# A hybrid encoder layer on eight cores: rewriting a phase-by-phase kernel as prioritised work streams, with a time-phased depthwise conv, a block-major last down pass, one weight ring and norm sums on VectorE

## What is computed

```python
x = x + 0.5 * swiglu(rmsnorm(x, ffn1_norm), ffn1_gate, ffn1_up, ffn1_down)     # hidden width 2816
z = rmsnorm(x, mix_norm) @ w_in                                               # 2560 columns
q, k, v, u = z[..., :512], z[..., 512:1024], z[..., 1024:1536], z[..., 1536:]
attn_out = chunk_band_attention(q, k, v, rel_bias)       # 8 heads of 64; 64-frame chunks see themselves and 8 before
g = u[..., :512] * sigmoid(u[..., 512:])
dw = causal_depthwise_conv(g, dw_kernel) + dw_bias       # 512 channels, 31 taps
conv_out = silu(layernorm(dw, conv_ln_g, conv_ln_b))     # norm over the channels
x = x + concat([attn_out, conv_out]) @ w_out
x = x + 0.5 * swiglu(rmsnorm(x, ffn2_norm), ffn2_gate, ffn2_up, ffn2_down)
y = rmsnorm(x, final_norm)
```

## Time and profile before

| what | us |
|---|---|
| median of 6 runs | 1756.24 (1752.36 to 1757.49) |
| the profiled execution | 1751.98 |
| its span on the slowest core (all cores: 1743.4 to 1750.4) | 1750.4 |
| TensorE busy | 1574.9 (90%) |
| VectorE busy | 569.3 (33%) |
| ScalarE busy | 459.0 (26%) |
| mean granted TensorE clock of the cores | 0.943 to 0.950 |

### The profile page before, as it was taken

One profiled execution on the slowest core, in us unless ns is written; L12 is line 12 of the kernel. 1 busy time (PEld: TensorE's weight loads), 2 busy tenths in 40 slices (PEclk: granted clock), 3 DMA queues, 4 the chain that ended last, 5 costly groups with the idle time before them and its releaser, 6 DMA issues.

```text
span 1750.4 us, 23671 instructions; the slowest of 8 cores (1743.4 to 1750.4 us)
## 1 busy us (share of the span) xinstructions
PE 1574.9 (90%) x8732; PEld 824.5 (47%) x8732; DVE 569.3 (33%) x1457; ACT 459.0 (26%) x874; POOL 47.8 (3%) x94
## 2 busy tenths in 40 slices
PE   4999999798877899959999998999898769999996
PEld 1555555344334455524555554444344435555552
DVE  3222222523444322243222223324354452222224
ACT  4110110313363311133110112223545351100113
POOL 0000000000000000000000000000000000000000
PEclk9999999899888899978999999899998969999998
DMA  9543324324000564661333232231000022333113
GB/s 224 85 72 61 55 49 79 85 49 73 1 1 10 88 103 85 111 171 49 65 59 65 49 73 49 42 66 31 1 1 1 1 48 49 70 63 55 25 27 124
DMA packets 14943, 105.68 MB, mean 60 GB/s; under 512 B 1648, under 2 KB 1776, under 8 KB 5872
## 3 DMA queue, kind: packets, MB, share of 16 engines
q0 software_dynamic: 12960, 83.89, 27.2%
q1 hardware_dynamic: 1872, 20.28, 3.3%
HBM read 179.66 MB, written 8.39 MB: 107 GB/s over the span
## 4 chain that ended last, share of the span: by engine, by line
PE 82%; DVE 6%; ACT 6%; DMA 3%; issue 3%; ACTq 0%; DVEq 0%; SPq 0%; POOLq 0%
PE ps L359 40%; PE ps L393 18%; PE ps L645 6%; PE ps L448 3%; PE ps L743 3%; PE ps L489 3%; PE ps L574 2%; DMA xres<-xin 2%; PE ps L467 2%; PE ps L600 2%; ACT sq L318 2%; PE ps L320 1%; DVE diag L629 1%; DVE scr L333 1%; DVE xres L333 1%
## 5 line engine op out<-in xcount | busy, mean ns | idle before, releaser
L359 PE MATMUL ps<-scr,gur 128*128 128x512 bf16 (+1 forms) x3872 | 693.0, 342 | 1.3 <-DVE scr L333 1.3
L359 PEld LDWEIGHTS ps<-scr,gur 128*128 128x128 bf16 x3872 | 380.1, 98 | 313.3 <-issue 10.0
L393 PE MATMUL ps<-scr,dr 128*128 128x512 bf16 (+1 forms) x1936 | 352.7, 344 | 2.7 <-DMA dr<-wdB 1.2
L367 ACT ACTIVATE scr<-ps 128x512 f32<-128x512 f32 (+1 forms) x242 | 125.7, 519 | 734.4 <-PE ps L359 734.4
L370 DVE TENSOR_TENSOR scr<-ps,scr 128x512 bf16<-128x512 f32 (+1 forms) x242 | 143.9, 595 | 534.4 <-PE ps L359 529.2
L393 PEld LDWEIGHTS ps<-scr,dr 128*128 128x128 bf16 x1936 | 189.9, 99 | 161.4 <-issue 7.6
L398 DVE SCALAR_TENSOR_TENSOR xres<-ps,xres 128x512 f32<-128x512 f32 (+1 forms) x176 | 103.9, 594 | 230.0 <-PE ps L393 229.9
L320 PE MATMUL ps<-sq,cb_sb 128*128 128x512 bf16 (+1 forms) x176 | 67.2, 409 | 87.8 <-ACT sq L318 83.9
L318 ACT ACTIVATE sq<-xres 128x512 bf16<-128x512 f32 (+1 forms) x176 | 88.1, 544 | 193.9 <-PE ps L320 137.6
L645 PE MATMUL ps<-g,diag 128*128 128x512 bf16 (+1 forms) x620 | 123.1, 361 | 5.9 <-DVE diag L629 5.9
L600 PE MATMUL ps<-scr,V 128*128 128x256 bf16 (+3 forms) x288 | 59.3, 309 | 48.3 <-DVE scr L616 22.9
(11 more groups left out here) (66 smaller groups left out, 570.4 us busy)
## 6 DMA issues: line engine op xcount, KB each, us to landing
gur<-wgu POOLq DMA_DIRECT2D x44, 1024.0 KB, 9.4
dr<-wdA POOLq DMA_DIRECT2D x16, 768.0 KB, 7.9
dr<-wdB POOLq DMA_DIRECT2D x16, 640.0 KB, 6.4
gur<-win POOLq DMA_DIRECT2D x10, 1024.0 KB, 9.4
xres<-xin SPq DMA_DIRECT2D x4, 2048.0 KB, 11.2
yout<-xres SPq DMA_DIRECT2D x3, 2048.0 KB, 6.3
gur<-wout POOLq DMA_DIRECT2D x4, 1024.0 KB, 9.5
xres<-xin SPq DMA_DIRECT2D x2, 1024.0 KB, 15.8
```

The source lines that it names most:

```text
L359: P.op("pe", lambda h, bank=bank, lhsT=lhsT, rhs=rhs, kc=kc: h.matmul(bank, lhsT=lhsT, rhs=rhs, start=(kc == 0), stop=(kc == 7)), reads=(( ...
L367: P.op("act", lambda h, tt=tt, gb=gb: h.activation(out=tt, in_=gb, func=AF.Silu), reads=(("ps", bG),), writes=(("tmpF", ti),))
L393: P.op("pe", lambda h, bank=bank, lhsT=lhsT, rhs=rhs, fl=fl, nf=nf: h.matmul(bank, lhsT=lhsT, rhs=rhs, start=(fl == 0), stop=(fl == nf - 1 ...
```

## The change

The kernel is written anew. Each phase is now a Python generator, a stream with a priority; `Sched.run` asks the streams in the order of priority whether their next piece of work can start by a planned time that `Prog` keeps for every engine (each operation comes with a planned duration), emits the first that can, or else the one that can soonest. The order on every engine is still fixed when the program is built.

- The passes' blocks are now 512, 384 and 384 frames (`GROUPS`). The second group's streams have priorities 10 lower in rank, so that its first feed-forward work can stand inside the first group's last.
- Conv: the gated values are written as four time phases (`gT`), 64 copies from SBUF to SBUF on SyncE's queue per group (32 on the way in, 32 back) bring 4 phases x 32 channels onto the partitions (`gp`), and 9 matmuls per 32 channels replace 31 per 128, each on a quarter of the frames. The weights for it (`wcv`) are made on the host and loaded like the others; nothing builds diagonals on VectorE. Its channel statistics lie on all phases at once, and a copy on VectorE brings the result back into time order (`cvt`).
- Norms: ScalarE squares each slice right behind the operation that completes it, VectorE adds the squares, one matmul with ones per block sums over the partitions.
- The last down part of each feed-forward runs block by block over all 8 output tiles. The final norm writes into a buffer of its own (`yb`), which is stored from there.
- Attention: the scores of two heads lie in four joined PSUM banks, and one exponential takes both heads; the streams of projections and of the output projection fill in.
- All weights go through one ring of 17,408 columns in the order of use. The first block of frames is loaded ahead of the weights, the other two behind the first weight piece.

```diff
-            for kc in range(8):
-                i = nxt("sq", 2)
...
-                P.op("pe", lambda h, bank=bank, sqt=sqt, kc=kc: h.matmul(
-                    bank, lhsT=onesS, rhs=sqt, start=(kc == 0), stop=(kc == 7)),
...
+GROUPS = (((512, True), (384, False), (384, False)),
+          ((512, False), (384, False), (384, False)))
...
+            now = self.P.t["pe"] + 0.1
+            best = None
+            for s in self.streams:
+                r = s[3]()
+                if r <= now:
+                    best = (r, s)
+                    break
+                if best is None or r < best[0]:
+                    best = (r, s)
...
+        def square(st, g, kc, s):
...
+            act(sqt, xsl(g, kc, s), AF.Square, n, (xk,), (("sq", i),))
+            if k < 7:
+                dve(lambda h: h.tensor_tensor(out=ss, in0=ss, in1=sqt, op=ALU.add), n,
+                    (("ssum", r), ("sq", i)), (("ssum", r),))
...
+                if hf == 0:
+                    order = [(dg, s, dm2) for dg in range(4) for s in blocks for dm2 in range(2)]
+                else:
+                    order = [(dg, s, dm2) for s in blocks for dg in range(4) for dm2 in range(2)]
...
+                for s4 in range(4):
+                    for j in range(4):
+                        src = gT[32 * j:32 * j + 32, 2 * pc:2 * pc + 2, s4, 0:W]
...
+            for grp in range(16):
+                p = wp[(gi, "cv%d" % (grp // 4))]
...
+                    if ("gp", gi) not in F or (grp > 1 and ("cstat", gi, grp - 2) not in F):
+                        return INF
...
+                for d in range(9):
+                    mm(b, 0, wv[:, grp % 4, d, :], gp[:, grp, 8 - d:8 - d + U], U, d == 0, d == 8,
+                       (("w", p.id), ("gp", grp), "gph"), d == 8)
...
+                act(abq[:, i, 0:U], a, AF.Copy, U, (("acc", grp),), (("abq", i),))
+                act(abq[:, i + 1, 0:U], a, AF.Square, U, (("acc", grp),), (("abq", i + 1),))
...
+            for grp in range(16):
+                gcol = cs[:, CS_LNG + grp:CS_LNG + grp + 1]
+                bcol = cs[:, CS_LNB + grp:CS_LNB + grp + 1]
+                act(co[:, grp, 0:U], acc[:, grp, 0:U], AF.Silu, U, (("acc", grp),), (("co", grp),),
+                    bias=bcol, scale=gcol)
...
+                    act(Pb[:, pi, :, 0:w], src, AF.Exp, 2 * w, (("ps", 2 * sp_), ("ps", 2 * sp_ + 1)), (("P", pi),))
...
+                def rdy0():
+                    if ("Q", gi, s) not in F or ("v", gi, s) not in F or ("ln45", gi) not in F:
+                        return INF
...
+        for g in G:
+            q = 10 * g.gi
+            S.add(q + 2, ffn(g, 0))
+            S.add(q + 3, glu(g))
+            S.add(q + 4, proj_k(g))
+            S.add(q + 5, attention(g))
+            S.add(q + 4.5, conv(g))
+            S.add(q + 6, proj_v(g))
+            S.add(q + 7, proj_q(g))
+            S.add(q + 8, wout(g))
+            S.add(q + 9, ffn(g, 1))
```

1588 lines of the change are left out of this document (902 added, 686 removed).

## The result

The changed kernel takes 1616.2 us (median of ten runs) against 1755.8 us of the kernel before: a ratio of 0.9205, 95% interval 0.9196 to 0.9215. That is faster, as forecast, but by 140 us and not by 263, and 56 us above the upper end of the range. The profiled execution took 1616.9 us, with a span of 1615.4 us on its slowest core. In some executions one die, or both, runs at a lower granted clock and the time is longer (one of 1730.8 us for this kernel); medians and comparisons leave these out.

A forecast was written before the change was run, and what follows sets the result against it. TensorE was taken as the bound. Start 27, feed-forward stretches 1059.8 and other stretches 401.4 us sum to a span of 1488 us, forecast as 1493 us, range 1430 to 1560 (about 0.8).

The forecast's parts named there:

- three signs of being wrong: Attention under 140 or over 190 us, a small copy's wait over 10 us, granted clock in attention below 0.75.
- parts 1 and 4: Conv in four time phases: 76 us of matrix work go; norm sums on VectorE: 65 us of matmuls become 3.9.
- part 5: Start: first block loaded alone, there after 9.5 us; 27 us lost until TensorE is continuous, against 33.7.
- parts 1 and 2: Conv in phases with hidden small copies, 10 us lost; SiLUs ahead of the value projection's evictions, 13 us lost.
- Part 2: Value projection: evictions stand behind 16 SiLUs in ScalarE's queue; stalls of 8 us in group 0, 5 in group 1.
- part 3: Attention with one exponential for two heads: 167 us with squares and a few evictions, bounds 126 and 190.
- part 4: Last down passes, norms on VectorE: VectorE becomes full, stalls 12 us over four passes, tail 13, reload hole 3.
- Rival 2: Attention: half clock for its head pairs, up to 85 us more, 1535 to 1580 us in all; chance 0.10.
- Rival 3: Last passes: VectorE does not catch up, SiLU and norm stalls reach upper bounds, 1520 to 1560 us; chance 0.06.
- Rival 4: Conv: the 128 small copies go one behind the other, slower than now from 2.85 us per copy; chance 0.03.
- Rival 5: Conv: TensorE waits for its weights every group, so 76 us less come off, 1569 us; chance 0.03.
- The likeliest case: Whole kernel: the forecast itself, 1440 to 1545 us; chance 0.66.

The follow-up runs named there:

- the first run of the section Together: Changed kernel plus squares as their own stream, block loads first in queue and plan, and values copied out of PSUM at once: 1572.1 us.
- the best run for each: Against the changed kernel: for the change of groups, second-group loads cut short, also in the plan, 1605.4 us; for the tail, norms multiplying half the columns, 1601.7 us.
- the best kernel of all: Changed kernel plus squares as own stream, loads first, values copied out at once, last down passes weight by weight, half the conv's first copies on GpSimd: 1549.7 us.

## Why the prediction was wrong, point by point

The terms for work held; the terms for lost time failed, 134 us forecast and 257 measured. The step that failed in most of them is the same: a wait was priced by itself, or taken as hidden, where the trace shows an instruction in an engine's queue that keeps back what stands behind it. The misses are 30 us at the change of groups, 26 in attention with its 15 us for the clock, 20 at the start, 19 in the first two last passes, 18 in conv and SiLUs and 10 in the tail. Of the three signs of being wrong that it set, two came: attention over 190 us and a wait for a small copy over 10 us.

**The work and the durations.** Right: 1354.4 us forecast, 1351.1 measured. The conv in phases and the statistics on VectorE are worth what parts 1 and 4 say in columns. The durations estimated from the earlier trace rows held too: 1.01 us for the joint exponential, 0.557 for an eviction of 384 columns, 0.613 for a norm's multiplication. No row of the kernel before has 384 columns, so what the prediction calls measured there are midway values. After, by shape:

```profile
L647 DVE SCALAR_TENSOR_TENSOR xres<-ps,xres 128x384 f32<-128x384 f32 x128 | 71.6, 560 | 97.3 <-PE ps L352 97.3
...
L356 ACT ACTIVATE dreg<-psA 128x1024 bf16<-128x1024 f32 x68 | 68.5, 1017 | 28.4 <-PE psA L352 26.4 <-PE ps L352 1.8
...
L506 DVE SCALAR_TENSOR_TENSOR hT<-xres,cs_sb,rstd 128x384 bf16<-128x384 f32 x96 | 51.9, 614 | 8.7 <-ACT rstd L356 8.7
```

**The start (part 5): 27 forecast, 47.3 measured.** Two steps failed. The rate of 0.3 MB per us came from a stretch with block loads alone; with weights on their way, which are float32 in memory and bfloat16 on arrival, the engines were full at 147 to 255 GB/s from 16 to 48 us (that the bytes read set this rate is not shown). And the second and third block were counted as ready on landing; their norms stood in ScalarE's queue behind the first block's SiLUs. With the loads early, the second step is 15 us. Both mended leaves 32.5 us, 5 above the forecast.

**Conv and SiLUs (parts 1 and 2): 23 forecast, 41.2 measured, and the step that failed is the copies', which were taken as hidden.** Issues of 0.46 us were taken from large loads; a small copy's took 0.82. The landing was left out: the last copy landed 13.6 us behind its issue, among weight pieces. And "hidden" overlooked that the copies' source is memory that the conv's evictions reuse. This is 10 us in group 0, with a wait of 13.39 us. Part 2's 13 us came out smaller. In group 1 TensorE waits 6.2 us just as it says (sixteen SiLUs in 8.83 us, then the eviction, then TensorE). In group 0 it waits 3.8 us, but the 3.04 of the first row below end with an eviction of VectorE's, which stood behind the LayerNorm's arithmetic on VectorE, and not behind SiLUs. (The split of 8 and 5 us does not follow from the prediction's own SiLU times either: with 0.54 us each in group 0 and 0.64 in group 1 the larger stall belongs to group 1.) Some 8 us of the 18 are not taken apart.

```profile
435.48 13.93 PE L352 MATMUL ps<-ring,hT 128*128 128x512 bf16 x56 [3.04 <-DVE vh L665]
...
1147.67 8.83 ACT L356 ACTIVATE dreg<-dreg,cs_sb 128x320 bf16<-128x320 f32 x16
1156.40 0.57 ACT L356 ACTIVATE at<-ps 128x512 bf16<-128x512 f32 x1
...
1157.12 8.61 PE L352 MATMUL ps<-hT,ring 128*128 128x512 bf16 x32 [6.01 <-ACT at L356]
```

**Attention (part 3): 167 forecast, upper bound 190; 206 measured** from the first score matmul to the last normalisation (78.1 + 128.2). The step that failed is the head pair's end. I let the next exponential cover it, but TensorE stands at the first value matmul, in order, until two logarithms, one exponential and two multiplications are through, about 2.9 us. And I counted the squares as ScalarE's time (13 us), not as a wait in its queue. Each mended alone, these two gave 24 and 17 us, and some 12 of the 24 are the lower clock behind the waits; with both mended (the first run of the section Together) the attentions lose 49 us (23.3 + 26.1), near the 41 of the forecast.

**Last passes (part 4): 6 forecast for the two first ones, 25.4 measured; tail 16 and 25.8.** The mechanism, eight multiplications ahead of the evictions, was right in part; that VectorE becomes full was not (40.40 of 69.60 us in the last stretch). Mis-sized were the stalls: 5.26 us where 3.3 were expected, and TensorE runs at the lower clock behind them. That the order is a gain at all was not questioned; undone, it gives 9 us. Half of the multiplications taken away give 14.5, though not by the evictions' waits alone. How the rest of the 25 us in the first two passes divides is not shown.

**Change of groups: 6 forecast, 35.8 measured.** The reload was taken as hidden but for 3 us. Only the first block is loaded early; the two others follow when their predecessors' norms are done. The second block's load lands about when its squares' turn in the queue comes, the third's 17 us before, and both are too late. Taking away load and place together gives 9 us; some 26 remain, and their cause is open.

**The rivals.** Rival 2, half clock in attention, holds in a small way: single stretches of 4 us do stand at 0.50, the 1.2 GHz level, with TensorE busy:

```profile
491.00:495.00 4.00, 3.66 (x23) 1.64 (x23) 1.11 (x2) 3.24 (x5) 0.00 (x0) 0.50 0.00 0
495.00:499.00 4.00, 4.00 (x25) 1.62 (x24) 0.00 (x0) 1.52 (x3) 0.00 (x0) 0.61 0.01 4
```

But on average 0.89 and 0.92 were granted, as before, and the price is about 18 us on the mean of six cores (21 on the slowest), not 40 to 85. What the Trainium skill says in TensorE: Matmul & The Clock Gate, section HAM oscillation, that bursts of matmuls between waits fall back to the half clock again and again, is seen here in part of the head pairs, with the 0.50 of the row above. Rival 3 named the place (the last passes), not the size. Rival 4's copies one behind the other did not come as such: the 64 of 40 KB landed after 1.9 us (median). But the 32 ahead of group 0's conv landed after 6.5, and the last of them held up the conv. The Trainium skill, DMA: Bandwidth & Descriptors, section Why small descriptors are slow, says that copies within SBUF are spared the penalty of small pieces; the 1.9 us do not speak against it, and no run here compares small pieces with large ones by themselves. Rival 5 did not come: TensorE's waits have no row for the conv's weights. The likeliest case fell because its stalls were priced one by one and small, and most were larger by what stands behind them.

**Still open:** 26 us at the change of groups and 20 of the tail are lost even in the best run for each, and 187 us in the best kernel of all.

## What to carry to other kernels

Count the work that a change removes and the time lost around it apart: the first can be had from columns to half a percent, the second does not go with it. In an order fixed by a planner, look for the instruction that waits in a queue with others behind it (a square, an eviction, a copy's issue), and price it with what stands behind it and with the lower clock after it, not with its own wait. And ask of a reordering meant to hide a step what the step now stands in front of.

## What the runs showed of the hardware

A VectorE product that writes its bfloat16 result in four interleaved streams takes 2400 ns for 512 columns; the same product with a contiguous result took 691 ns in the kernel before. The two kernels' rows, after and before:

```profile
L720 DVE TENSOR_TENSOR dreg<-psA,dreg 128x512 bf16<-128x512 f32 x4 | 9.6, 2400 | 5.3 <-ACT dreg L356 2.7 <-PE psA L352 2.7
```

```profile
L499 DVE TENSOR_TENSOR g<-ps,scr 128x512 bf16<-128x512 f32 x12 | 8.3, 691 | 40.2 <-ACT scr L496 40.2
```

It is 39.5 us of VectorE in all; none of TensorE's waits ends with it (no row for L720). The issue of a 32-partition copy within SBUF held SP for 0.82 us (mean of 32) and GpSimd's queue for 0.53 (mean of 8). Beside weight loads such a copy of 25 KB landed 6.5 us after its issue (median of 32), and the last one after 13.6.
